# Another order of residual adds and low parts where a stage of a two-block network begins

## Chip, cores and metric

The kernel runs on one core of a Trainium2 chip. The metric is the device time of one launch in microseconds (us), as the median of several runs. TensorE is called PE below, VectorE DVE, ScalarE ACT, GpSimd POOL, SyncE SP.

## What is computed

A sequence of 256 tokens with 1024 features passes through two blocks of two layers each, all in float32. Each layer is

```
x = x + 0.5 * swiglu(rms_norm(x, g1), w_in1, w_out1)
x = x + mixer(rms_norm(x, g2), ...)
x = x + 0.5 * swiglu(rms_norm(x, g3), w_in3, w_out3)
```

`swiglu` is `(silu(h @ w_gate) * (h @ w_up)) @ w_out` with 2816 hidden features. The mixer of the first block is neighbourhood attention and a Fourier mix, both gated; that of the second block joins three kinds of attention. The first block ends with one more `rms_norm`.

## The kernel before

There are twelve stages, numbered n = 0 to 11: feed-forward (n mod 3 = 0), mixer (1), feed-forward (2), for two layers of each block. The activations `x` stay in SBUF, transposed: 8 chunks of 128 features by 256 tokens, `s.x[:, k]`.

A float32 product is made of three matmuls in a faster format: every operand is split into a high part (a rounding, by ACT) and a low part (the value less its high part, by DVE). For weights, `Stream` loads slots of three 128x1024 tiles, a front pair and a back one, two slots deep. ACT rounds them (`round_hi`, L89; `round_half`, L98), DVE makes the low part (`rest`, L111; `rest_half`, L120), and the semaphore that DVE raises (`split`) lets PE use the slot and SP load the next one over it (`load`, L72).

A stage is entered before its norm is known. The gains go into the activations at once, the inverse root mean square is applied behind the first product. At an entry three engines work together.

- DVE, `enter` (L430): five residual adds `add(0)` to `add(4)` (L426), which take the last stage's output out of PSUM into `x`. They cover chunks 0, 1, 2-3, 4-5 and 6-7. Then, for each chunk k, `low(k)` (L443), the low part of the activations, which waits for ACT's high part of the same chunk. Each `low(k)` raises `xl_ready`.
- ACT, `lead_scalar` (L366 on): for each chunk, once its add is done, the high part (L382); after each second chunk the squares of the two (L300).
- PE: `wait_x` (L558) for chunk k, then the matmuls with it. In a feed-forward, `ffn_first` (L593) does three products at a time for each chunk (gate and up of the first slot, gate of the second: L571 and L576), and after them the up product of the second slot. In front of the last chunk it does `mean_squares` (L524), matmuls that sum the squares over the features. They wait for DVE's `add_squares` (L499, L502), which DVE does behind the entry. In the first-block mixer `wide_part` uses each chunk in turn (L213 to L215), two chunks to a weight tile; DVE makes the low part of the third tile (the first back slot, L111) right behind `enter`, and the sums after it. In the second-block mixer `add_squares` comes right behind `enter`. Only stage n = 6 sums its squares by PE alone (`joint_squares`, L540).

Each engine works through its own program in order, so at an entry the order written in `enter` is DVE's order. `ffn_vector` makes the low part of the second slot's front tile in two halves. The first comes ahead of `enter`; the second (`second_half`) comes ahead of `enter` too at n = 2, 5, 8, 11, and is passed to `enter` as `between` at n = 3, 6, 9. Mixers (L1194, L1911) pass nothing. Stage 0 has an entry of its own, `first_enter`.

Of the kernel before, what the change touches and what calls it, by code (L numbers as in the profile page):

```python
# [19 lines left out]
KD = D // P  # L20
# [395 lines left out]
def residual(s, w, n, j, came):  # L416


    base, slot, c, factor = came
    c0, c1 = SUMS[j]  # L420
    if c1 < KD:
        s.nc.vector.wait_ge(s.y_bank, 3 * (n - 1) + (c1 + 1) // 2)
    else:
        w.wait_taken(s.nc.vector, base, slot, c)
    xs = s.x[:, c0:c1].rearrange("p k t -> p (k t)")
    s.nc.vector.scalar_tensor_tensor(xs, y_region(s, c0, c1), factor, xs, ALU.mult,  # L426
                                     ALU.add).then_inc(s.x_ready, 1)


def enter(s, w, n, came, between=None):  # L430


    nc, dve = s.nc, s.nc.vector
    g = s.gains[n]

    def add(j):
        if n == X2 + 1 and j == 0:
            dve.wait_ge(s.rescaled, KD)
        residual(s, w, n, j, came)

    def low(k):
        dve.wait_ge(s.xh_ready, KD * n + k + 1)
        nc.vector.scalar_tensor_tensor(s.xl[:, k], s.x[:, k], g[:, k:k + 1],  # L443
                                       s.xh[:, k].bitcast(F32), ALU.mult, ALU.subtract).then_inc(
            s.xl_ready, 1)

    add(0)
    add(1)
    if between is not None:
        between()  # L450
    low(0)
    add(2)
    low(1)
    add(3)
    low(2)
    low(3)
    add(4)
    for k in range(4, KD):
        low(k)


# [261 lines left out]
def ffn_vector(s, w, base, slot0, n, f, came):  # L723
# [54 lines left out]
    if n == 0:  # L778
        first_enter(s, w)
        add_squares(s, n)  # L780
        w.rest_half(nc.vector, 1, 1, 0, s.half_hi, 1, s.half_split)
        inverse(s, n)
        w.rest_half(nc.vector, 1, 1, 1, w.hi_done[0], 2, w.split[0])
    else:
        slot1 = base + slot0 + 1
        w.rest_half(nc.vector, slot1, 1, 0, s.half_hi, HALF_AT[n] + 1, s.half_split)

        def second_half():
            w.rest_half(nc.vector, slot1, 1, 1, w.hi_done[0], slot1 + 1, w.split[0])

        if n % 3 == 2:
            second_half()
        enter(s, w, n, came, None if n % 3 == 2 else second_half)
        if n == X2:
            move_on(dve, s.sums_ready, 4 * n, 4)
        else:
            add_squares(s, n)
# [387 lines left out]
def mix1_vector(s, m, mark, w, base, slot0, n, layer):  # L1185
# [5 lines left out]
    def split(slot):  # L1191
        w.split_pair(nc.vector, base, slot0 + slot)

    enter(s, w, n, (base, slot0 - 1, 2, 0.5))  # L1194
    w.rest(nc.vector, 1, base + slot0, 0)
    w.rest(nc.vector, 0, base + slot0 + 1, 1)
# [695 lines left out]
def mix2_vector(s, m, mark, w, base, slot0, n, layer):  # L1892
# [16 lines left out]
    slot1 = base + slot0 + 1  # L1909
    w.rest_half(nc.vector, slot1, 1, 0, s.half_hi, HALF_AT[n] + 1, s.half_split)  # L1910
    enter(s, w, n, (base, slot0 - 1, 2, 0.5))  # L1911
    add_squares(s, n)
    w.rest(nc.vector, 1, base + slot0, 0)
# [684 lines left out]
```

## Time and profile before

| | |
|---|---|
| median of 3 runs | 2321.6 us (2319.95 to 2322.09) |
| profiled execution, its own time | 2322.34 us |
| its span | 2320.5 us, 42273 instructions |
| PE busy | 2293.7 us, 99% |
| DVE busy | 1834.5 us, 79% |
| ACT busy | 1151.1 us, 50% |
| mean granted TensorE clock | 0.997 of full speed |
| DMA | 407.61 MB, 51.0% of 16 engines |
| front weight load, median from issue to landing | 4.9 us |

How to read it: busy is the time in which an engine had an instruction under way. PE is busy nearly throughout, DVE and ACT have idle time that counts only where PE waits for them. Times in the rows below are microseconds from the start of the span, then the duration, so an instruction ends at the sum of the two; an engine's next one may start a little before that.

### The profile page before, as it was taken

How to read it: one execution, taken by the hardware profiler on the slowest of the kernel's cores; microseconds unless marked ns; L12 is line 12 of the kernel's file. 1: busy time of each engine (PE TensorE's matmuls, PEld its weight loads, DVE VectorE, ACT ScalarE, POOL GpSimd, SP SyncE). 2: the span in 40 equal slices, each digit the busy share in tenths (PEclk: the TensorE clock that was granted, in tenths of full speed). 3: DMA queues.
4: the chain of work that ended last, by engine and by line, in shares of the span. 5: the costliest groups of instructions: out<-in, count | busy, mean ns of one | idle time of the engine just before them, and what ended most of it. 6: DMA issues, size and time to landing. Idle time of an engine off the chain costs nothing.

```text
span 2320.5 us, 42273 instructions
## 1 busy us (share of the span) xinstructions
PE 2293.7 (99%) x16096; PEld 2096.2 (90%) x16096; DVE 1834.5 (79%) x2987; ACT 1151.1 (50%) x1533; POOL 4.8 (0%) x10
## 2 busy tenths in 40 slices
PE   8999999999999999999999999999999999999999
PEld 7998999999998999999999888999999997889998
DVE  7788468788878568877878878888798787878877
ACT  5445465445335465435434665654354456665443
POOL 0000000000000000000000000000000000000000
PEclk9999999999999999999999999999999999999999
DMA  6555445555555435554655432455545545234654
GB/s 241 187 188 206 157 141 194 185 188 175 197 187 202 160 123 199 200 187 146 211 187 194 164 136 110 164 191 190 190 171 189 184 173 191 86 134 166 215 183 133
DMA packets 76383, 407.61 MB, mean 176 GB/s; under 512 B 9216, under 2 KB 9872, under 8 KB 43776
## 3 DMA queue, kind: packets, MB, share of 16 engines
q1 hardware_dynamic: 75936, 405.78, 51.0%
q8 instruction: 64, 1.05, 0.2%
q0 software_dynamic: 208, 0.49, 0.1%
q14 instruction: 31, 0.25, 0.0%
q10 hardware_dynamic: 144, 0.04, 0.0%
HBM read 405.23 MB, written 1.05 MB: 175 GB/s over the span
## 4 chain that ended last, share of the span: by engine, by line
PE 94%; DVE 3%; ACT 1%; issue 1%; DMA 0%; SPq 0%; DVEq 0%; ACTq 0%
PE ps_aux L571 14%; PE ps_proj L571 14%; PE ps_y L213 10%; PE ps_y L215 10%; PE ps_y L214 10%; PE ps_proj L576 7%; PE ps_aux L576 7%; PE ps_proj L213 5%; PE ps_proj L215 5%; PE ps_proj L214 5%; PE ps_y L1659 1%; PE ps_aux L1692 1%; ACT w_hi_front L89 1%; PE ps_y L1670 1%; DVE w_lo_back L111 0%
## 5 line engine op out<-in xcount | busy, mean ns | idle before, releaser
L111 DVE TENSOR_TENSOR w_lo_front<-w_raw_front,w_hi_front 128x2048 fp32r<-128x2048 f32 x242 | 553.3, 2286 | 58.3 <-ACT w_hi_front L89 56.1
L89 ACT CAST w_hi_front<-w_raw_front 128x2048 fp32r<-128x2048 f32 x242 | 461.5, 1907 | 191.1 <-PE ps_aux L571 161.2
L571 PE MATMUL ps_proj<-xt_lo_hi,w_hi_front 128*128 128x512 f32 x1408 | 511.8, 394 | 10.1 <-DVE w_lo_front L139 9.1
L571 PE MATMUL ps_aux<-xt_lo_hi,w_hi_front 128*128 128x512 f32 x1408 | 511.9, 394 | 0.8 <-DVE w_lo_front L139 0.8
L213 PE MATMUL ps_y<-hidden_lo,w_hi_back 128*128 128x256 f32 x1408 | 397.0, 282 | 0.9 <-DVE hidden_lo L761 0.3
L215 PE MATMUL ps_y<-hidden_hi,w_hi_back 128*128 128x256 f32 x1408 | 396.6, 282 | 0.0
L214 PE MATMUL ps_y<-hidden_hi,w_lo_back 128*128 128x256 f32 x1408 | 396.0, 281 | 0.0
L576 PE MATMUL ps_aux<-xt_lo_hi,w_lo_front 128*128 128x256 f32 x1408 | 371.6, 283 | 0.0
L576 PE MATMUL ps_proj<-xt_lo_hi,w_lo_front 128*128 128x256 f32 x1408 | 369.2, 282 | 0.0
L89 ACT CAST w_hi_back<-w_raw_back 128x1024 fp32r<-128x1024 f32 x252 | 264.6, 1050 | 191.5 <-PE ps_y L215 149.1
L701 ACT ACTIVATE silu_gate<-silu_gate 128x256 f32<-128x256 f32 x176 | 73.6, 418 | 493.8 <-DVE silu_gate L738 493.8
L571 PEld LDWEIGHTS ps_proj<-xt_lo_hi,w_hi_front 128*128 128x128 f32 x1408 | 264.9, 188 | 57.5 <-issue 9.0
L111 DVE TENSOR_TENSOR w_lo_back<-w_raw_back,w_hi_back 128x1024 fp32r<-128x1024 f32 x252 | 307.1, 1219 | 5.4 <-ACT w_hi_back L89 4.9
L571 PEld LDWEIGHTS ps_aux<-xt_lo_hi,w_hi_front 128*128 128x128 f32 x1408 | 264.8, 188 | 48.4 <-DVE w_lo_front L139 1.3
L576 PEld LDWEIGHTS ps_aux<-xt_lo_hi,w_lo_front 128*128 128x128 f32 x1408 | 265.1, 188 | 14.7
L576 PEld LDWEIGHTS ps_proj<-xt_lo_hi,w_lo_front 128*128 128x128 f32 x1408 | 265.5, 189 | 7.0
L214 PEld LDWEIGHTS ps_y<-hidden_hi,w_lo_back 128*128 128x128 f32 x1408 | 265.0, 188 | 6.1
L213 PEld LDWEIGHTS ps_y<-hidden_lo,w_hi_back 128*128 128x128 f32 x1408 | 264.7, 188 | 2.9 <-issue 2.9
L215 PEld LDWEIGHTS ps_y<-hidden_hi,w_hi_back 128*128 128x128 f32 x1408 | 265.2, 188 | 0.0
L732 DVE TENSOR_REDUCE silu_gate<-ps_proj 128x256 f32<-128x512 f32 x176 | 121.5, 691 | 139.7 <-PE ps_proj L571 139.7
L744 DVE TENSOR_REDUCE hidden<-ps_aux 128x256 f32<-128x512 f32 x176 | 121.5, 690 | 72.6 <-PE ps_aux L571 72.6
L213 PE MATMUL ps_proj<-xn_lo_hi,w_hi_front 128*128 128x256 f32 x512 | 149.7, 292 | 0.0
(394 smaller groups left out, 3720.2 us busy)
## 6 DMA issues: line engine op xcount, KB each, us to landing
w_raw_front<-in_stream SPq DMA_DIRECT2D x252, 1024.0 KB, 4.9
w_raw_back<-in_stream SPq DMA_DIRECT2D x252, 512.0 KB, 3.6
m_rel_bias<-in_rel_bias SPq DMA_DIRECT2D x2, 2048.0 KB, 8.2
m_params<-in_params SPq DMA_DIRECT2D x2, 656.0 KB, 4.3
x<-in_x SPq DMA_DIRECT2D x4, 256.0 KB, 6.0
w_raw_front<-in_stream SPq DMA_DIRECT2D x2, 512.0 KB, 6.0
out<-x SPq DMA_DIRECT2D x3, 256.0 KB, 2.2
m_dft_time<-in_dft_t POOLq DMA_DIRECT2D x1, 256.0 KB, 3.9
```

The lines of the kernel that those rows point to most:

```text
L89: self.nc.scalar.copy(self.hi[part][:, parity], self.raw[part][:, parity]).then_inc(self.hi_done[part], 1)
L111: eng.tensor_tensor(self.lo[part][:, parity], self.raw[part][:, parity], self.hi[part][:, parity].bitcast(F32), ALU.subtract).then_inc(sel ...
L213: nc.tensor.matmul(out, ah, bl, start=start, stop=False)
L214: nc.tensor.matmul(out, al, bh, start=False, stop=False)
L215: return nc.tensor.matmul(out, ah, bh, start=False, stop=stop)
L571: return nc.tensor.matmul(bank[:], hi[:, cols], s.xlh[:, k].rearrange("p j t -> p (j t)"), start=k == 0, stop=k == KD - 1)
L576: last = nc.tensor.matmul(bank[:, 0:T], lo[:, cols], s.xh[:, k], start=False, stop=False)
L701: nc.scalar.activation(at, at, ACT.Silu).then_inc(s.silu_done, 1)
L732: nc.vector.tensor_reduce(s.act[:, p], s.pj[p][:].rearrange("p (j t) -> p t j", j=2), AX.X, ALU.add).then_inc(s.gate_added, 1)
L744: nc.vector.tensor_reduce(s.hid[:, p], s.pa[p][:].rearrange("p (j t) -> p t j", j=2), AX.X, ALU.add).then_inc(s.up_added, 1)
L1659: mark.inc(nc.tensor.matmul(s.py[step % 2][:, 0:2 * kw], m.qT[:, qc, i * P:(i + 1) * P], m.kbd[:, kv, :, 0:kw]), "scores_done")
L1670: last = nc.tensor.transpose(s.py[2 + b][:, j * P:(j + 1) * P], m.scs[job % 3][:, j * P:(j + 1) * P], s.ident[:])
```

## The change

`enter` gets another order, for all stages but the first. The low parts of chunks 0 and 1 come together, then the adds of chunks 2-3 and 4-5 together, then low parts 2 and 3. The `between` step of n = 3, 6, 9 moves from behind the second add to behind the low part of the fourth chunk. The low part of chunk 4 moves ahead of the last add. Nothing is added or left out.

```diff
     add(0)
     add(1)
-    if between is not None:
-        between()
     low(0)
+    low(1)
     add(2)
-    low(1)
     add(3)
     low(2)
     low(3)
+    if between is not None:
+        between()
+    low(4)
     add(4)
-    for k in range(4, KD):
+    for k in range(5, KD):
         low(k)
```

## Rows read from the trace of the kernel before

**Rows 1.** The page, engines: busy us (share), instructions.
```profile
PE 2293.7 (99%) x16096; PEld 2096.2 (90%) x16096; DVE 1834.5 (79%) x2987; ACT 1151.1 (50%) x1533; POOL 4.8 (0%) x10
```

**Rows 2.** Waits of PE: us in total, times, longest.
```profile
PE ps_proj L571 <- DVE xt_lo_hi L443: 1.0, 3, 0.3
```

**Rows 3.** Timeline of DVE, entry n = 2: start, duration, engine, line.
```profile
358.83 0.76 DVE L426 SCALAR_TENSOR_TENSOR x<-ps_y,x 128x256 f32<-128x256 f32 x2
359.84 0.48 DVE L443 SCALAR_TENSOR_TENSOR xt_lo_hi<-x,params_all,xt_lo_hi 128x256 fp32r<-128x256 f32 x1 [0.25 <-ACT xt_lo_hi L382]
360.24 0.69 DVE L426 SCALAR_TENSOR_TENSOR x<-ps_y,x 128x512 f32<-128x512 f32 x1
...
363.22 1.81 DVE L443 SCALAR_TENSOR_TENSOR xt_lo_hi<-x,params_all,xt_lo_hi 128x256 fp32r<-128x256 f32 x4
364.95 2.28 DVE L499 TENSOR_TENSOR squares<-squares 128x512 f32<-128x512 f32 x3
367.26 0.43 DVE L502 TENSOR_TENSOR squares<-squares 128x256 f32<-128x256 f32 x1
```

**Rows 4.** Timeline of ACT, entry n = 2.
```profile
359.29 0.51 ACT L382 ACTIVATE xt_lo_hi<-x,params_all 128x256 fp32r<-128x256 f32 x1
...
360.96 0.51 ACT L382 ACTIVATE xt_lo_hi<-x,params_all 128x256 fp32r<-128x256 f32 x1 [0.23 <-DVE x L426]
...
362.30 0.49 ACT L382 ACTIVATE xt_lo_hi<-x,params_all 128x256 fp32r<-128x256 f32 x1
...
363.62 0.50 ACT L382 ACTIVATE xt_lo_hi<-x,params_all 128x256 fp32r<-128x256 f32 x1
```

**Rows 5.** Timeline of PE, stage n = 2.
```profile
368.13 0.50 PE L524 MATMUL ps_y<-ones,squares 128*128 128x1 f32 x4
```

**Rows 6.** Timeline of DVE, entry n = 3.
```profile
545.83 0.76 DVE L426 SCALAR_TENSOR_TENSOR x<-ps_y,x 128x256 f32<-128x256 f32 x2
546.50 1.22 DVE L120 TENSOR_TENSOR w_lo_front<-w_raw_front,w_hi_front 128x1024 fp32r<-128x1024 f32 x1
547.63 0.48 DVE L443 SCALAR_TENSOR_TENSOR xt_lo_hi<-x,params_all,xt_lo_hi 128x256 fp32r<-128x256 f32 x1
...
552.74 2.28 DVE L499 TENSOR_TENSOR squares<-squares 128x512 f32<-128x512 f32 x3
555.05 0.42 DVE L502 TENSOR_TENSOR squares<-squares 128x256 f32<-128x256 f32 x1
```

**Rows 7.** Timeline of PE, stage n = 3.
```profile
547.65 0.28 PE L215 MATMUL ps_y<-hidden_hi,w_hi_back 128*128 128x256 f32 x1
548.26 0.47 PE L571 MATMUL ps_proj<-xt_lo_hi,w_hi_front 128*128 128x512 f32 x1 [0.33 <-DVE xt_lo_hi L443]
548.57 0.28 PE L576 MATMUL ps_proj<-xt_lo_hi,w_lo_front 128*128 128x256 f32 x1
...
555.72 0.50 PE L524 MATMUL ps_y<-ones,squares 128*128 128x1 f32 x4
```

**Rows 8.** Timeline of SP's queue, stage n = 3.
```profile
547.90 0.33 SPq L72 DMA_DIRECT2D w_raw_front<-in_stream  x1
```

**Rows 9.** Timeline of ACT, stage n = 3.
```profile
559.17 1.89 ACT L89 CAST w_hi_front<-w_raw_front 128x2048 fp32r<-128x2048 f32 x1
```

**Rows 10.** Timelines of DVE and PE, stage n = 1, first-block mixer.
```profile
204.05 1.22 DVE L111 TENSOR_TENSOR w_lo_back<-w_raw_back,w_hi_back 128x1024 fp32r<-128x1024 f32 x1
...
205.24 0.40 PE L215 MATMUL ps_proj<-w_hi_front,xt_lo_hi 128*128 128x512 f32 x1
205.47 0.39 PE L213 MATMUL ps_proj<-w_lo_back,xt_lo_hi 128*128 128x512 f32 x1
```

**Rows 11.** Timelines of DVE and PE, stage n = 7, second-block mixer.
```profile
1280.47 0.42 DVE L502 TENSOR_TENSOR squares<-squares 128x256 f32<-128x256 f32 x1
...
1281.38 0.50 PE L524 MATMUL ps_y<-ones,squares 128*128 128x1 f32 x4
```

**Rows 12.** Stretch in a mixer: us, busy of each engine, PEclk, DMA, GB/s.
```profile
1347.00:1353.50 6.50, 6.50 (x32) 6.50 (x32) 3.33 (x5) 1.23 (x3) 0.00 (x0) 0.50 0.51 179
```

## The prediction

> **What bounds the kernel.** I read the page's first part, the PE waits, then the timelines of each engine at the entries. PE is busy 99% of the span [rows 1]: whatever delays its instruction stream lengthens the run, and whatever else the change moves costs nothing. The waits give the entries (lines 430 to 459) a small stake: PE waited for `xt_lo_hi` of L443 three times, 1.0 us in all [rows 2]. There are eleven entries, n = 1 to 11: four before a second feed-forward (n = 2, 5, 8, 11), two before a first-block mixer (1, 4), two before a second-block mixer (7, 10), and three before a first feed-forward (3, 6, 9), the only ones that pass a `between`. The timelines of n = 2, 3, 1 and 7 stand in the rows. The same offsets repeat in the others.
>
> **Where the three waits come from.** At n = 3 the adds start at 545.83, then the half-width low part L120 (1.22 us) runs at 546.50, and only then `low(0)` at 547.63, ending 548.11 [rows 6]. PE's last down matmul starts at 547.65 and the next, in a stream that goes on every 0.12 us, would start at 547.77. It starts at 548.26, 0.15 us after `low(0)` ended, and the matmul behind it follows after 0.31 us [rows 7] where 0.23 us is usual behind 512 columns (205.24 to 205.47 [rows 10]). So the gap costs 0.49 + 0.08 = 0.57 us, three times.
>
> **What the change removes.** With nothing between, `low(0)` starts 1.01 us after the first add (359.84 against 358.83 at n = 2 [rows 3]), so at n = 3 at 546.84, ending 547.32: before PE is done with its down matmuls. PE gets the first chunk without a wait. Each chunk feeds 1.07 us of matmuls (seven in the 7.46 us from 548.26 to 555.72 [rows 7]), and the low parts come every 0.4 to 1.2 us, so no later `wait_x` of a feed-forward is late either. Gain at the start of each of these three stages: 0.57 us.
>
> **What the change delays.** Behind the low parts on VectorE come the adds of squares (L499, L502), which PE needs for `mean_squares` (L524) in the middle of its stream. All entries get the new order, so this counts eleven times. I work it out in offsets from the first add, with the durations of n = 2 [rows 3, 4]. Issue distances on VectorE: 0.40 after a low part, 0.60 after a 512-wide add. A ScalarE cast starts 0.03 us after the add it needs has ended (360.24 + 0.69 = 360.93, cast 360.96), a low part 0.04 us after its cast (359.29 + 0.51 = 359.80, low part 359.84). ScalarE goes from the third cast to the fifth in 1.34 us and to the seventh in 2.66 (360.96, 362.30, 363.62).
> Before: third cast at +2.13, low parts 4 to 7 from +4.39 and `add(4)` 0.60 ahead of them at +3.79, the adds of squares start at +6.12 (364.95).
> After: `low(0)` +1.01, `low(1)` +1.41, `add(2)` +1.81, ending +2.50. Third cast +2.53, fifth cast +3.87, ending +4.37, so `low(4)` waits until +4.41, where VectorE was free at +3.88. The last add is queued behind this wait: `add(4)` runs at +4.81 instead of +3.79 and ends at +5.49. ScalarE could have made the seventh cast at +5.19, now at +5.52, ending +6.02; `low(6)` +6.06, `low(7)` +6.46, adds of squares +6.86. That is 0.74 us later than before. Nobody asked for `add(2)` and `add(3)` sooner: they even slip by 0.4 and 0.0 us.
> At n = 3, 6, 9 the half-width part (issue distance 1.13) fills the hole ahead of `low(4)`: `low(3)` +3.48, the half +3.88, `low(4)` +5.01, `add(4)` +5.41, ending +6.09, seventh cast +6.12 to +6.62, `low(6)` +6.66, squares +7.46. Before they started at +6.91 (552.74 against 545.83 [rows 6]): 0.55 us later.
>
> **What that costs on PE**, by the distance of 0.15 us from a producer's end to a waiting matmul, and 0.08 for the slow step behind it:
> - n = 2, 5, 8, 11: L502 ends at 367.26 + 0.43 = 367.69 [rows 3]; late by 0.74 it lets L524 start at 368.58. It started at 368.13 [rows 5], in its turn. 0.45 + 0.08 = 0.53 each, 2.12 in all. What follows (root, reciprocal, diagonal, SiLU, hidden) hangs on this matmul and on the same VectorE queue and comes late by as much, not more.
> - n = 3, 9: L502 ended 555.05 + 0.42 = 555.47 [rows 6], 0.10 us ahead of need for L524 at 555.72 [rows 7]. Now 556.02 + 0.15 = 556.17: 0.45 + 0.08 = 0.53 later than before, although the stage began 0.57 sooner. The gain is lost in a new wait of about 1.0 us. Together 1.06.
> - n = 6 sums its squares on PE (L540) without VectorE's adds, and ScalarE's squares have over 2 us to spare there. The gain stays: -0.57.
> - n = 1, 4: the low part of the first back slot (L111) comes right behind the entry: 204.05 to 205.27. PE's first matmul with it is at 205.47 [rows 10]. Now 206.01 + 0.15 = 206.16: 0.69 + 0.08 = 0.77 each, 1.54 in all. The sums come later in this stage and shift with PE.
> - n = 7, 10: L502 ends 1280.89, L524 at 1281.38 [rows 11]. Now 1281.63 + 0.15 = 1281.78: 0.40 + 0.08 = 0.48 each, 0.96 in all; for n = 10 this is an estimate from n = 7.
> Sum: 2.12 + 1.06 - 0.57 + 1.54 + 0.96 = 5.1 us later.
>
> **What I cost at nothing.** The half's `split` is signalled about 3.3 us later at n = 3, 6, 9, and SP's next front load waits for it (issued at 547.90 [rows 8]), with the back load queued behind it, which waits longer anyway for L111 of the back slot. Issued near 551.2 and landing 4.9 us later, near 556.1, it is cast at 559.17 [rows 9]: 3 us of cover. Were it gone, ScalarE and then PE would wait for whatever exceeds it. The half itself is needed by the up product, after the 8.4 us of the first three products. PE's own waits deep in the mixers come from chains that start at PE, so they give nothing back; the granted clock sits at 0.50, 1.2 of 2.4 GHz, for 6.5 us in one mixer [rows 12], and such a stretch is worth some 3.3 us if it came or went.
>
> **Bounds.** The hidden side: the trace does not show how late PE would be if it had to wait at L524, only that it does not. If a matmul can start 0.05 instead of 0.15 us after its producer and without the slow step, the ten entries that lose cost about 0.18 less each: 3.3 us in all. If the casts and low parts do not pack again behind the longer wait (another 0.15 us hole each), they add 1.5: 6.6. If all the lateness fell beside work, the least is -1.7 (three gains of 0.57). I take 5.1, the value by the rows of waits that PE does have.
>
> The profiled execution took 2322.34 us (2320.5 of span, 1.8 around it). With the sum it would take 2327.4. The median of the runs is 2321.6, 0.7 lower, so I predict 2326.7.
>
> **Rivals.**
> 1. The gain stays and nothing new is late: PE starts sooner at n = 3, 6, 9 and the sums still come in time. For it speaks that no wait at L524 is listed. Against: the margin at n = 3 is 0.10 us. Time 2321.6 - 1.7 = 2319.9; it decides if the order cost VectorE less than 0.1 us. The Trainium skill, Perfetto Trace Analysis, section Optimization Strategy, points this way: find the gap on the most contended engine, find which semaphore it waited on, and make that dependency start sooner. By that rule alone the change is right; the trace agrees about the gap, but the rule doesn't ask what else the same engine has queued. Chance 0.10.
> 2. Half hidden: only the places with almost no margin pay (n = 1, 4, 3, 9: 2.6 us less 0.57), because `low(4)`'s wait overlaps the hop differently and the shift is nearer 0.3 us. Time 2321.6 + 2.0 = 2323.6. The margins of 0.29 at n = 2 and 0.34 at n = 7 allow it, the arithmetic of the offsets speaks against. Chance 0.22.
> 3. More than reckoned: a hole of 0.15 us more each, or a new clock stretch at 1.2 GHz behind one of the stalls. Against the clock: the stall of 0.5 us at n = 3 was followed by a normal pace, 1.07 us a chunk. 2328 to 2331. Chance 0.08.
> My forecast has 0.60.
>
> **How the numbers follow.** A change of 0.2% (4.6 us) is about what a measurement of this kernel can tell. The forecast case runs from 2325.3 to 2328.2, some three quarters of it above 2326.2; with rival 3 that makes 0.55 for slower. Same takes the rest of it and rivals 1 and 2, 0.42. Faster needs a mechanism I don't see, such as both slow-clock stretches going away: 0.03. The range, 2321.5 to 2329, leaves out rival 1 and the top of rival 3.
>
> **What would show it.** In the changed kernel: at n = 3, 6, 9 no idle time ahead of the first L571, which starts 0.12 us after the last L215; a VectorE hole of half a microsecond ahead of the fifth low part at n = 2; L499 starting 6.86 us after the first add at n = 2 and 7.46 at n = 3; waits of PE L524 for DVE L502 at eight entries (all but 1, 4 and 6), and of L213 for `w_lo_back` L111 at n = 1 and 4. I am wrong if L499 keeps its offset, or if PE shows those waits and the whole is still not longer.

## The result and the profile after

The changed kernel took 2325.62 us (median of 12 runs, 2324.07 to 2327.98), the kernel before 2321.25 (12 runs, 2319.86 to 2322.5): ratio 1.0021, 95% interval 1.0013 to 1.0028. It is slower, by 4.4 us by the medians where 5.1 were forecast (2326.7), and the interval lies wholly above 1. The profiled execution took 2326.28 us, its span was 2324.5. One kernel's runs differ by its granted clock: of 30 later runs of the kernel before, 19 took 2319.95 us on average at a mean granted clock of 0.998 and 11 took 2322.01 at 0.997, so its median was 2321.25 here and 2320.17, 2320.10 and 2321.21 in the later batches, by the mix of the two.

In the changed kernel the lines behind `enter` have moved by one: L525 is the old L524, L500 and L503 the adds of squares, L572 the first products. Four of the waits of PE, in us in total, times and longest:

```profile
PE ps_y L525 <- DVE squares L503: 2.4, 6, 0.8
PE ps_aux L572 <- DVE w_lo_front L139: 1.1, 1, 1.1
PE ps_proj L213 <- DVE w_lo_back L111: 0.9, 2, 0.4
PE ps_y L213 <- DVE hidden_lo L762: 0.3, 1, 0.3
```

The wait for `xt_lo_hi` [rows 2] is gone and two new ones, for the sums and for the mixer's back weights, have come. The six waits at L525 are those of n = 2, 3, 5, 8, 9 and 11. At n = 7 and 10 PE waits for the sums too, 0.15 and 0.07 us, too short for this list: there too L525 starts 0.05 us after the sums end. The timeline of DVE at n = 2, to set beside [rows 3]:

```profile
360.08 0.76 DVE L426 SCALAR_TENSOR_TENSOR x<-ps_y,x 128x256 f32<-128x256 f32 x2
361.08 0.88 DVE L443 SCALAR_TENSOR_TENSOR xt_lo_hi<-x,params_all,xt_lo_hi 128x256 fp32r<-128x256 f32 x2 [0.25 <-ACT xt_lo_hi L382]
361.88 1.28 DVE L426 SCALAR_TENSOR_TENSOR x<-ps_y,x 128x512 f32<-128x512 f32 x2
363.14 0.89 DVE L443 SCALAR_TENSOR_TENSOR xt_lo_hi<-x,params_all,xt_lo_hi 128x256 fp32r<-128x256 f32 x2
364.46 0.48 DVE L443 SCALAR_TENSOR_TENSOR xt_lo_hi<-x,params_all,xt_lo_hi 128x256 fp32r<-128x256 f32 x1 [0.44 <-ACT xt_lo_hi L382]
364.87 0.68 DVE L426 SCALAR_TENSOR_TENSOR x<-ps_y,x 128x512 f32<-128x512 f32 x1
365.47 0.47 DVE L443 SCALAR_TENSOR_TENSOR xt_lo_hi<-x,params_all,xt_lo_hi 128x256 fp32r<-128x256 f32 x1
366.13 0.89 DVE L443 SCALAR_TENSOR_TENSOR xt_lo_hi<-x,params_all,xt_lo_hi 128x256 fp32r<-128x256 f32 x2 [0.18 <-ACT xt_lo_hi L382]
366.93 2.27 DVE L500 TENSOR_TENSOR squares<-squares 128x512 f32<-128x512 f32 x3
369.24 0.43 DVE L503 TENSOR_TENSOR squares<-squares 128x256 f32<-128x256 f32 x1
```

The brackets show both holes: 0.44 us ahead of `low(4)`, and 0.18 ahead of `low(6)`, whose cast waited for the last add. L500 starts 6.85 us after the first add. At n = 3, beside [rows 6], the moved half fills the first hole and the second stays; L500 is at +7.46:

```profile
547.54 0.75 DVE L426 SCALAR_TENSOR_TENSOR x<-ps_y,x 128x256 f32<-128x256 f32 x2
551.41 1.22 DVE L120 TENSOR_TENSOR w_lo_front<-w_raw_front,w_hi_front 128x1024 fp32r<-128x1024 f32 x1
552.54 0.48 DVE L443 SCALAR_TENSOR_TENSOR xt_lo_hi<-x,params_all,xt_lo_hi 128x256 fp32r<-128x256 f32 x1
554.20 0.89 DVE L443 SCALAR_TENSOR_TENSOR xt_lo_hi<-x,params_all,xt_lo_hi 128x256 fp32r<-128x256 f32 x2 [0.18 <-ACT xt_lo_hi L382]
555.00 2.27 DVE L500 TENSOR_TENSOR squares<-squares 128x512 f32<-128x512 f32 x3
```

PE at n = 2, n = 3 and n = 1, beside [rows 5, 7, 10]. In n = 3 PE goes from the last L215 to the first L572 in 0.12 us, and pays for it at L525:

```profile
369.72 0.61 PE L525 MATMUL ps_y<-ones,squares 128*128 128x1 f32 x4 [0.19 <-DVE squares L503]
...
549.36 0.28 PE L215 MATMUL ps_y<-hidden_hi,w_hi_back 128*128 128x256 f32 x1
549.48 0.39 PE L572 MATMUL ps_proj<-xt_lo_hi,w_hi_front 128*128 128x512 f32 x1
...
557.79 0.61 PE L525 MATMUL ps_y<-ones,squares 128*128 128x1 f32 x4 [0.77 <-DVE squares L503]
...
206.57 0.50 PE L213 MATMUL ps_proj<-w_lo_back,xt_lo_hi 128*128 128x512 f32 x1 [0.44 <-DVE w_lo_back L111]
```

The lengths of the stages, each from its first residual add (L426) to that of the next, changed kernel less the one before, from the timelines of DVE:

| stage n | forecast, us | profile, us |
|---|---|---|
| 1, 4 | +0.77 each | +0.74, +0.68 |
| 2, 5, 8, 11 | +0.53 each | +0.46, +0.55, +0.50, +0.63 |
| 3, 9 | +0.53 each | +0.58, +0.55 |
| 6 | -0.57 | -0.58 |
| 7, 10 | +0.48 each | -1.23, +0.55 |

Only n = 7 is off, by 1.7 us. There the time came back from the granted TensorE clock. In this mixer PE waits 3.20 us at L1570 (L1571 in the changed kernel), and soon after the clock falls to half for a while. Before, it fell 0.54 us after the end of the wait and stayed at 0.50 (1.2 of 2.4 GHz) for 6.83 us; in the changed kernel it fell 1.03 us after the end and stayed there for 3.41 us. Nearly the whole of the two stretches, before and after (columns as in [rows 12]):

```profile
1346.85:1353.65 6.80, 6.80 (x34) 6.80 (x33) 3.33 (x5) 1.38 (x3) 0.00 (x0) 0.50 0.53 192
```

```profile
1350.70:1354.08 3.38, 3.38 (x18) 3.38 (x18) 3.21 (x5) 0.99 (x1) 0.00 (x0) 0.50 0.50 204
```

PE is busy throughout both, so 3.41 us less at half speed give 1.7 us back. The other ten stages sum to +4.66. With n = 7 at its forecast it would be 5.1. Stage 0, which the change does not touch, was 0.50 us longer in this execution (PE waited 0.5 us more for the first weights), and 4.66 - 1.23 + 0.50 is the 3.9 us by which the two profiled executions differ.

Why n = 3 lost although PE began it 0.57 us sooner shows in two lines of DVE, behind the sums. The low part of a weight tile (L111) comes first and then the reciprocal of the norm (L510, L511 in the changed kernel), from which the diagonal, SiLU and the first down matmul follow. Before, and then in the changed kernel:

```profile
555.40 1.22 DVE L111 TENSOR_TENSOR w_lo_back<-w_raw_back,w_hi_back 128x1024 fp32r<-128x1024 f32 x1
556.55 0.17 DVE L510 RECIPROCAL inv_rms<-rms 128x2 f32<-128x2 f32 x1
```

```profile
557.65 1.22 DVE L111 TENSOR_TENSOR w_lo_back<-w_raw_back,w_hi_back 128x1024 fp32r<-128x1024 f32 x1
558.79 0.16 DVE L511 RECIPROCAL inv_rms<-rms 128x2 f32<-128x2 f32 x1
```

Both times the reciprocal starts as L111 ends, 10.72 us after the first add before and 11.25 after. It had no margin on DVE even before the change, so PE's earlier start could not shorten this stage.

### The profile page after: what moved, and what is told of

It reads as the page before. It is cut to its first block, busy times and chain, and to the rows that moved or that the text cites. A ratio compares the mean times of both kernels' runs of the same rounds, so it can differ in the third digit from the quotient of the medians.

```text
span 2324.5 us, 42273 instructions
## 1 busy us (share of the span) xinstructions
PE 2294.7 (99%) x16096; PEld 2095.0 (90%) x16096; DVE 1834.8 (79%) x2987; ACT 1152.1 (50%) x1533; POOL 4.8 (0%) x10
## 4 chain that ended last, share of the span: by engine, by line
PE 90%; DVE 5%; ACT 2%; issue 1%; DMA 0%; SPq 0%; DVEq 0%; ACTq 0%
PE ps_aux L572 14%; PE ps_proj L572 13%; PE ps_y L213 10%; PE ps_y L215 10%; PE ps_y L214 10%; PE ps_aux L577 7%; PE ps_proj L577 7%; PE ps_proj L213 5%; PE ps_proj L215 5%; PE ps_proj L214 5%; DVE xt_lo_hi L443 1%; PE ps_y L1660 1%; ACT xt_lo_hi L382 1%; DVE x L426 1%; DVE squares L500 1%
## 5 line engine op out<-in xcount | busy, mean ns | idle before, releaser
L111 DVE TENSOR_TENSOR w_lo_front<-w_raw_front,w_hi_front 128x2048 fp32r<-128x2048 f32 x242 | 553.1, 2286 | 58.9 <-ACT w_hi_front L89 56.6
L572 PE MATMUL ps_proj<-xt_lo_hi,w_hi_front 128*128 128x512 f32 x1408 | 511.5, 393 | 9.3 <-DVE w_lo_front L139 9.3
L572 PE MATMUL ps_aux<-xt_lo_hi,w_hi_front 128*128 128x512 f32 x1408 | 512.0, 394 | 1.1 <-DVE w_lo_front L139 1.1
L213 PE MATMUL ps_y<-hidden_lo,w_hi_back 128*128 128x256 f32 x1408 | 397.0, 282 | 0.8 <-DVE hidden_lo L762 0.3
L215 PE MATMUL ps_y<-hidden_hi,w_hi_back 128*128 128x256 f32 x1408 | 396.6, 282 | 0.0
L572 PEld LDWEIGHTS ps_proj<-xt_lo_hi,w_hi_front 128*128 128x128 f32 x1408 | 264.9, 188 | 56.1 <-issue 9.3
L111 DVE TENSOR_TENSOR w_lo_back<-w_raw_back,w_hi_back 128x1024 fp32r<-128x1024 f32 x252 | 306.8, 1218 | 4.8 <-ACT w_hi_back L89 4.0
L572 PEld LDWEIGHTS ps_aux<-xt_lo_hi,w_hi_front 128*128 128x128 f32 x1408 | 264.8, 188 | 48.5 <-DVE w_lo_front L139 1.6
L213 PEld LDWEIGHTS ps_y<-hidden_lo,w_hi_back 128*128 128x128 f32 x1408 | 264.7, 188 | 2.8 <-issue 2.8
L215 PEld LDWEIGHTS ps_y<-hidden_hi,w_hi_back 128*128 128x128 f32 x1408 | 265.2, 188 | 0.0
L213 PE MATMUL ps_proj<-xn_lo_hi,w_hi_front 128*128 128x256 f32 x512 | 149.6, 292 | 0.0
```

Of the source, the lines that this page charges most:

```text
L111: eng.tensor_tensor(self.lo[part][:, parity], self.raw[part][:, parity], self.hi[part][:, parity].bitcast(F32), ALU.subtract).then_inc(sel ...
L213: nc.tensor.matmul(out, ah, bl, start=start, stop=False)
L215: return nc.tensor.matmul(out, ah, bh, start=False, stop=stop)
L572: return nc.tensor.matmul(bank[:], hi[:, cols], s.xlh[:, k].rearrange("p j t -> p (j t)"), start=k == 0, stop=k == KD - 1)
```

## Experiments

An offset is a time counted from a stage's first add, in the profiled execution; without more words it is that of L499, the first add of squares. A hole is idle time of DVE, a "half" the `between` step of n = 3, 6, 9. My theory: what a stage costs is set by DVE's offset at L499 (and, at n = 1 and 4, at L111), and the order makes that offset late through two holes. Rivals: the moved half is what hurts; the pairing of the first low parts is; DVE's order hurts whatever ACT does; only PE's waiting at L524 counts. Each kernel below has the edit shown, against the kernel before unless it says otherwise. "n = 6: -0.59" means that this stage is 0.59 us shorter than in the kernel before. In stages that an edit does not reach these lengths repeat within 0.05 us, but for n = 1 (up to 0.28) and n = 6, 7 and 10, where the clock can differ from trace to trace (last section).

**The half alone**

```diff
     add(0)
     add(1)
-    if between is not None:
-        between()
     low(0)
     ...
     low(3)
+    if between is not None:
+        between()
     add(4)
```

> One part of the change alone: the between step moves behind the low part of the fourth chunk, the adds and low parts keep the order of before. My theory (VectorE's offset at L499 sets the cost): nothing changes at n = 1, 2, 4, 5, 7, 8, 10, 11. At n = 6 the stage is 0.57 us shorter. At n = 3 and 9 PE starts 0.57 us sooner, but the wait for the first cast, which the half-width part covered before, is open again, so L499 starts at about +7.12 instead of +6.91 and the stage ends 0.1 to 0.2 us later than before. In all -0.3 us, ratio 0.9999. Rival (it is the moved half that delays the sums): at n = 3 and 9 L499 comes at +7.46 as in the changed kernel, each 0.5 us longer, in all +0.5 us. Rival (the starting gap is all that counts): three times -0.57, in all -1.7 us.

Ratio 0.9998 (0.9989 to 1.0007). n = 6: -0.59; n = 3: +0.23; n = 9: +0.18; all others but the mixer n = 10 (-0.10) within 0.04. The adds of squares of n = 3, DVE:

```profile
545.72 0.76 DVE L426 SCALAR_TENSOR_TENSOR x<-ps_y,x 128x256 f32<-128x256 f32 x2
546.72 0.48 DVE L443 SCALAR_TENSOR_TENSOR xt_lo_hi<-x,params_all,xt_lo_hi 128x256 fp32r<-128x256 f32 x1 [0.25 <-ACT xt_lo_hi L382]
...
552.82 2.28 DVE L499 TENSOR_TENSOR squares<-squares 128x512 f32<-128x512 f32 x3
```

+7.10, neither +7.46 (the rival) nor +6.91: before, the half lay in the 0.25 us hole of `low(0)`, which is now open. A start 0.57 us sooner was turned into an end 0.2 us later, twice, and kept where DVE makes no sums. Neither rival's time came: +0.5 and -1.7 in all were forecast, the stages sum to -0.3.

**The order alone** (the changed kernel, `between` back behind `add(1)`)

```diff
     add(0)
     add(1)
+    if between is not None:
+        between()
     low(0)
     ...
     low(3)
-    if between is not None:
-        between()
     low(4)
```

> The other part alone: adds and low parts in the new order, with the low part of chunk 4 ahead of the last add, and the between step left behind the second add. My theory: every entry but n = 6 loses as in the changed kernel or more: n = 1, 4: 0.7 each; n = 2, 5, 8, 11: 0.55 each; n = 7, 10: 0.5 each; n = 3, 9: L499 at +7.66 instead of +6.91, 0.65 to 0.7 each; n = 6: 0. In all +6.0 us, ratio 1.0026. Rival (the moved half is what costs): +0 to +1.

Ratio 1.0027 (1.0017 to 1.0038): the order alone is the whole loss and more. L500, the old L499, is at +6.85 and, with the half, +7.65; n = 1, 4: +0.75, +0.72; n = 2, 5, 8, 11: +0.45, +0.49, +0.49, +0.64; n = 3 and 9 are +0.72 and +0.73, n = 6 -0.02. The mixer n = 7 again had the shorter slow stretch (-1.25).

**The last add put back** (the changed kernel with one exchange)

```diff
-    low(4)
     add(4)
-    for k in range(5, KD):
+    for k in range(4, KD):
```

> The changed kernel with one exchange undone: the last add goes ahead of the low part of chunk 4 again (at n = 3, 6, 9 behind the between step). My theory (the last add is queued behind the wait of the low part of chunk 4, and ScalarE's seventh cast behind it): without half, L499 at +6.53 instead of +6.86 (before +6.12), with half +7.21 instead of +7.46. Stages against before: n = 1, 4: +0.4 each; n = 2, 5, 8, 11: +0.2; n = 7, 10: +0.1; n = 3, 9: +0.2 to +0.3; n = 6: -0.57. In all +1.9 us, ratio 1.0008. Rival (the pairing of the first low parts, which makes the third chunk's add late, is the cause): the offsets stay at +6.86 and +7.46 and the time at +4.4 us.

Ratio 1.0007 (0.9998 to 1.0016), an interval that does not reach the rival's +4.4 us. Offsets +6.51 and, with the half, +7.18. n = 1, 4: +0.38, +0.35; n = 2, 5, 8, 11: +0.16, +0.19, +0.12, +0.26; n = 3, 9: +0.30, +0.22. DVE at n = 2: no hole ahead of `low(4)`, and the one ahead of `low(6)` is there because ACT's own casts come no sooner.

```profile
359.54 0.76 DVE L426 SCALAR_TENSOR_TENSOR x<-ps_y,x 128x256 f32<-128x256 f32 x2
...
363.41 0.68 DVE L426 SCALAR_TENSOR_TENSOR x<-ps_y,x 128x512 f32<-128x512 f32 x1
364.01 0.87 DVE L443 SCALAR_TENSOR_TENSOR xt_lo_hi<-x,params_all,xt_lo_hi 128x256 fp32r<-128x256 f32 x2
365.25 0.89 DVE L443 SCALAR_TENSOR_TENSOR xt_lo_hi<-x,params_all,xt_lo_hi 128x256 fp32r<-128x256 f32 x2 [0.37 <-ACT xt_lo_hi L382]
366.05 2.27 DVE L499 TENSOR_TENSOR squares<-squares 128x512 f32<-128x512 f32 x3
```

Here n = 6 came out +1.01 instead of -0.57, n = 7 -1.57 and n = 10 -1.40 instead of +0.1; the clock again, see the last section. The eight other stages sum to +2.0, where 2.0 to 2.2 were forecast.

**`low(4)` ahead of the last add, nothing else**

```diff
     low(3)
+    low(4)
     add(4)
-    for k in range(4, KD):
+    for k in range(5, KD):
```

> Only the smallest part of the change: the low part of chunk 4 goes ahead of the last add, all else as before. My theory: ScalarE's fifth cast ends at +3.97, so this low part waits until +4.01 where VectorE was free at +3.79, the last add follows at +4.41 (before +3.79), and L499 starts at +6.46 (before +6.12). n = 1, 4: +0.3 each; n = 2, 5, 8, 11: +0.1 to +0.2; n = 7, 10: 0 to +0.1; n = 3, 9: +0.3 to +0.4; n = 6: 0. In all +1.8 us, ratio 1.0008. Rival (pairing the low parts is the whole cause): 0.

Ratio 1.0013 (1.0004 to 1.0022). Offset +6.46 at n = 2; n = 1, 4: +0.34, +0.31; n = 2, 5, 8, 11: +0.09, +0.11, +0.13, +0.23; n = 3, 9: +0.33, +0.30; n = 6: 0.00; n = 7, 10: -0.67 and -1.38, the clock. So the two edits of the order cost about the same: 0.34 of offset by this one, 0.39 by the pairing (the kernel above, +6.51 against +6.12), and together 0.73. The pairing is half of the cause, since it makes the third chunk's add, and with it all of ACT's later casts, 0.4 us late; it is not the whole.

**ACT's order changed under DVE's new one** (the changed kernel)

```diff
-        if k % 2 == 1:
+        if k in (1, 7):
             squares(s, n, k // 2)
+        if k == 5:
+            squares(s, n, 1)
+            squares(s, n, 2)
```

> The changed kernel, but ScalarE makes the high parts of chunks 4 and 5 ahead of the squares of chunks 2 and 3 (both squares follow the sixth chunk's high part). VectorE's order stays that of the changed kernel. My theory (the hole is the low part of chunk 4 waiting for its cast, with the last add behind it): the fifth cast ends 0.5 us sooner, at +3.84, the hole ahead of the low part of chunk 4 is gone, the last add runs at +4.28 instead of +4.81, and L499 starts at +6.53 instead of +6.86 without half; with half, nothing was waited for there, L499 stays near +7.3 to +7.46. Time as in the kernel with the last add put back: 2.1 us less than the changed kernel, +2 us against before, ratio 1.0009. Rival (VectorE's order itself costs, whatever ScalarE does): no change against the changed kernel, ratio 1.002.

Ratio 1.0014 (1.0005 to 1.0023). The first add of squares is at +6.51 without the half, +7.47 with it; n = 2, 5, 8, 11: +0.15, +0.19, +0.16, +0.25, as with the last add put back, while n = 3, 9 stay at +0.57, +0.54. The time as a whole does not decide (the interval holds both forecasts, 1.0009 and 1.002, and n = 10 was -1.36 by its clock); the offset does. ACT at n = 2, four casts in a row (L429 is the add, L426 elsewhere):

```profile
360.39 0.91 ACT L382 ACTIVATE xt_lo_hi<-x,params_all 128x256 fp32r<-128x256 f32 x2
361.20 0.61 ACT L300 ACTIVATE squares<-x 128x512 f32<-128x512 f32 x1
362.45 1.71 ACT L382 ACTIVATE xt_lo_hi<-x,params_all 128x256 fp32r<-128x256 f32 x4 [0.63 <-DVE x L429]
364.07 1.14 ACT L300 ACTIVATE squares<-x 128x512 f32<-128x512 f32 x2
```

DVE's order was not touched, and at n = 2 its delay was nearly halved, from 0.73 to 0.39 us. The order hurts through the casts it waits for.

**The mixer's back weights ahead of the wait** (the changed kernel)

```diff
-    enter(s, w, n, (base, slot0 - 1, 2, 0.5))
-    w.rest(nc.vector, 1, base + slot0, 0)
+    enter(s, w, n, (base, slot0 - 1, 2, 0.5),
+          lambda: w.rest(nc.vector, 1, base + slot0, 0))
```

> The changed kernel, but at n = 1 and 4 the low part of the first back slot (L111) is made in the between place, behind the low part of the fourth chunk. My theory (these two stages are longer because this low part follows the entry and PE wants it 7.5 us after the first add): the low part is there at about +5.1, PE no longer waits for it, the part fills the wait ahead of the low part of chunk 4, and both stages have their length of before: 1.4 us less than the changed kernel, +3.0 us against before, ratio 1.0013. Rival (these stages are longer because the sums of squares or the low parts of the activations are late for PE): nothing changes against the changed kernel, +4.4 us.

n = 1 and 4 are +0.02 and -0.03 where the changed kernel has +0.74 and +0.68, though the low parts of the activations come even later than there (the last at +7.06 instead of +6.45). The sums of squares are no rival: in the changed kernel they end at +12.93 in this stage and PE takes them up at +13.81, without a wait. So the low part of the back weights was the whole loss of these two stages. The time as a whole doesn't decide it: ratio 1.0018 (1.0009 to 1.0027), which holds both forecasts; in the profile n = 6 and n = 10 had other clocks (+0.98 and -1.07), and n = 7 that of the changed kernel (-1.23).

**PE asks for the sums one chunk later** (the changed kernel)

```diff
-        elif k == KD - 2:
+        elif k == KD - 1:
             mean_squares(s, n)
```

> The changed kernel, with PE's mean_squares behind the last chunk's matmuls instead of ahead of them, so that PE has 1.07 us of work more before it asks for the sums. Theory A (PE's waiting at L524 is the whole cost, what follows has slack): the wait goes, and the six feed-forward stages n = 2, 3, 5, 8, 9, 11 become 0.45 us shorter each, 2.7 us less than the changed kernel. Theory B (the hidden product hangs on the chain root, reciprocal, diagonal, SiLU, and that chain starts at L524): L524 comes 0.6 to 0.8 us later than in the changed kernel, the first down matmul L213 waits for hidden_lo by as much, and these six stages are 0.6 to 0.8 us longer, some 4.5 us more than the changed kernel, +9 us against before, ratio 1.0038. I hold B.

Ratio 1.0035 (1.0023 to 1.0047), 8.3 us by the medians. Two of the waits of PE:

```profile
PE ps_aux L1571 <- ACT silu_gate L1811: 6.4, 2, 3.2
PE ps_y L550 <- ACT hidden L320: 5.0, 6, 0.9
```

The waits at L525 are gone and one link down, at L550 (`spread_rows`), PE waits 5.0 us for the diagonal: theory B. Against the changed kernel n = 2, 5, 8, 11 are 0.55, 0.50, 0.53 and 0.40 longer. At n = 3 and 9 nothing changed (-0.04, -0.03), which I had wrong: the sums there were so late that L525 moved by 0.12 us only, +10.37 against +10.25, and the reciprocal did not move at all (+11.25 in both), since it starts as L111 ends on DVE. At n = 2 it moved from +10.64 to +11.18, and the stage by as much. So theory B has to be put more narrowly: a stage follows the reciprocal, which waits for the later of two things, the sums' way over PE and ACT and DVE's own queue. By the lengths the edit cost 1.9 us more than the changed kernel and not 4.5; that the total came near the forecast of +9 is in part the mix of clocks.

**An order without holes**

```diff
     add(0)
     add(1)
-    if between is not None:
-        between()
-    low(0)
     add(2)
+    low(0)
     low(1)
     add(3)
     low(2)
     low(3)
     add(4)
+    if between is not None:
+        between()
```

> An order meant to leave VectorE no hole: adds 0, 1 and 2, low parts 0 and 1, add 3, low parts 2 and 3, add 4, the between step, then low parts 4 to 7. My theory: the third add fills the wait for the first cast, the casts then come in time. L499 at +5.79 instead of +6.12 without half, at +6.81 instead of +6.91 with it; first low part at +1.31, still before PE needs it. n = 6: -0.57, n = 3, 9: -0.2 to -0.3 each, the others 0, because PE's matmuls ahead of L524 take their time anyway. In all -1.1 us, ratio 0.9995. Rival (each microsecond VectorE gains at an entry shortens the stage): eight entries times -0.33 more, -3.7 us. Rival (the later first low part costs PE): 0.3 us longer at each entry, +2 us.

Ratio 0.9999 (0.9990 to 1.0008). The offsets came as reckoned, +5.76 and +6.82, 0.36 and 0.09 sooner than before. It bought nothing at n = 2, 5, 8, 11 (+0.09, +0.08, +0.08, +0.11): PE's own matmuls set L524, and a first low part 0.3 us later costs 0.1 us at the start. n = 6: -0.49; n = 3, 9: -0.10 each, less than I wrote and just what the offset gained. The first rival's -3.7 us and the second's +2 did not come.

**What the runs point to**

```diff
     low(3)
+    if n == X2:
+        between()
     add(4)
     ...
         last_up = by_both(s, s.pa[0], up0, k)
+        if n % 3 == 2 and k == KD - 2:
+            mean_squares(s, n)
     ...
     for k in range(KD):
+        if n % 3 == 2 and k == 0:
+            spread_rows(s, n)
         last = by_both(s, s.pa[1], up1, k)
```

(X2 is n = 6; the calls in their old places then skip these stages.) PE sums the squares one product earlier at n = 2, 5, 8, 11, and spreads the inverse root ahead of the last product instead of a chunk into it.

> The kernel before with what the runs point to: the between step is put off at n = 6 alone, where no sums of VectorE hang on it; and at n = 2, 5, 8, 11 PE sums the squares one product earlier (ahead of the second slot's gate product of the seventh chunk) and spreads the inverse root one chunk earlier, since the sums were there 0.29 us ahead of need and the first down matmul waited 0.25 us for the hidden product. My theory: n = 6: -0.57. n = 2, 5, 8, 11: L524 at +8.95 to +9.0 instead of +9.3, the reciprocal, now held by VectorE's queue, 0.2 us earlier, so that the wait for the hidden product shrinks by 0.2: -0.2 each. In all -1.4 us, ratio 0.9994. Rival (the chain behind L524 isn't what the first down matmul waits for): only -0.57, ratio 0.9998.

2319.66 us against 2321.21, ratio 0.9997 (0.9988 to 1.0006): not to be told from no change, and the interval holds both forecasts, though it is clearly not the changed kernel's loss. In the profile n = 6 is -0.54, n = 2, 5, 8 are -0.15, -0.14, -0.19, n = 11 -0.02, some 1.0 us in all where 1.4 were forecast. At n = 2 the low part of the hidden product ended 0.23 us sooner, but PE's first down matmul started only 0.08 sooner: now its own matmuls ahead set it. Of the stages that the edit does not reach, n = 7 is -1.66 by its clock, and n = 1 and 10 are -0.25 and -0.39 for reasons that the runs do not show.

## Why the prediction was right

- **The start at n = 3, 6, 9.** Forecast: PE passes from L215 to the first product in 0.12 us. It does. The gain of 0.57 was kept only at n = 6 (-0.58, and -0.59 with the half alone). The step that was taken at no cost, the next front load of the weights, held: at n = 3 it was issued 5.27 us after the first add instead of 2.07, and ACT did not wait for it.
- **The hole ahead of `low(4)` with the last add behind it.** Forecast offsets +6.86 and +7.46, measured +6.85 and +7.46. `low(6)` was forecast at +6.06 and is at +6.05.
- **The cost at L524.** n = 2: forecast 0.53, measured 0.46; n = 3: 0.53 and 0.58. The distance from the end of the sums to the matmul was taken as 0.15 us from another wait; here it was 0.05 (369.24 + 0.43 = 369.67, L525 at 369.72), but the four small matmuls then took 0.61 instead of 0.50. By these two L524 would cost 0.34 + 0.11 = 0.45 at n = 2, and 0.36 + 0.11 = 0.47 at n = 3. At n = 3 the rest was luck: the stage follows the reciprocal, 0.53 later, and that follows DVE's queue. In all nine experiments and in the changed kernel n = 3 and 9 changed by what the offset of L499 changed, within 0.05 us. The trace of the kernel before had both distances, 0.15 us at L571 and 0.05 at L1570; what decides between them was not settled.
- **n = 1, 4.** Forecast 0.77, measured 0.74 and 0.68, again by other terms: L213 starts 0.05 us after L111 ends, 0.59 later than before, and the step behind it is 0.11 us longer. Only the experiment with the back weights showed that this wait, not a later one, was the loss.
- **Rivals.** "The gain stays" fell at n = 3 and 9, with the half alone: the move opened a hole of 0.25 us, and the reciprocal behind it had no margin at all, where the prediction counted 0.10 us at L524. "Half hidden" fell with the offsets. "More than reckoned" did not come either: the changed kernel's profile shows no new slow stretch. Of the eight waits for the sums that the prediction asked for, six are listed and two are shorter than the list shows. The rule that makes the waited-for dependency start sooner (the Trainium skill, Perfetto Trace Analysis, Optimization Strategy) held for one stage of three: n = 6 gave 0.59 us, n = 3 and 9 took 0.2 each.
- **What was costed at nothing** and moved is the n = 7 mixer's clock, 1.7 us to the good in the profiled execution. The prediction had named such a stretch as a risk without saying which way. The sum of 5.1 was right without it. The medians, 4.4, hold different clocks in different executions; the kernel before alone moves its median by 1.1 us from batch to batch, so the 0.7 us between them and the sum say nothing against the sum and are not assigned.
- **The chain.** That nothing behind L524 has slack was argued from the queue; the kernel with the later sums showed it for n = 2, 5, 8, 11. At n = 3 and 9 what has no slack is DVE's queue up to the reciprocal.

## What to carry to other kernels

An in-order engine that serves several consumers has one currency: the offset of each thing in its queue. Before moving an instruction with a wait ahead of another, look up when its producer will be ready, and which producers wait for the one now behind it; a hole of 0.44 us ahead of `low(4)` became two. And when the wait at the head of a stage is removed, follow the chain to the next places where the engines meet and look at the margin of each: here 0.10 us by the prediction's count at the sums, and none at the reciprocal, against 0.57 of gain.

## What the runs showed of the hardware

Of the granted TensorE clock between the first microseconds and the end of the kernel, the eleven traces show this: it is 1.00 but for short stretches at 0.50, one in each second-block mixer (n = 7 and 10), and in two traces one more at n = 6.

In the mixers PE waits 3.20 us at L1570, and the clock falls between 1.3 us ahead of the end of that wait and 1.9 us behind it. In all 22 cases the length goes with that moment: 6.83 us where the fall came at most 0.54 us behind the end of the wait (12 cases), 3.41 us where it came 0.62 us or more behind it (10 cases). The first costs some 3.4 us of PE's time and the second 1.7, less where part of the stretch falls into the wait: so the -0.67 at n = 7 with `low(4)` alone. So kernels with the same work in these mixers came out up to 1.7 us apart there, by the moment at which the clock fell. This is read from the traces; no experiment set the moment on purpose. The two groups of runs of the kernel before, 2 us apart, differ by about as much; that they have the same cause is not shown.

In the n = 6 stage, where PE sums the squares with two-column matmuls, nine traces show full speed and two 0.94 over 30 us, a stretch of 3.41 us at 0.50 that begins as the last of these matmuls ends, with PE busy all the time ahead of it. The kernel before, and the one with the last add put back:

```profile
1080.00:1110.00 30.00, 29.67 (x204) 27.35 (x203) 23.17 (x40) 16.52 (x30) 2.33 (x2) 1.00 0.32 109
```

```profile
1080.00:1110.00 30.00, 30.00 (x197) 27.63 (x196) 22.35 (x42) 18.34 (x32) 2.33 (x2) 0.94 0.36 120
```

That stage was then +1.01 instead of about -0.58, 1.6 us. These 1.4 to 1.7 us apiece are as large as most effects studied here, which is why the stage lengths, not the total, decide between the theories. What makes the clock fall at n = 6 in some executions and not in others was not settled.
